# Gated linear attention: operands and outputs moved four chunks at a time, the samples' steps placed between the chunks

## The chip, the core and the metric

The kernel runs on one core of a Trainium2 chip. A core has TensorE (PE), VectorE (DVE), ScalarE (ACT), GpSimd (POOL) and SyncE (SP); each works through its own list of instructions and waits on semaphores for the others. SP, ACT and POOL issue DMAs. The metric is the device time of one execution in microseconds, lower is better.

## What is computed

The whole program is one inference step of two layers for 2048 prompt tokens and 8 sample tokens. The part at issue is the gated linear attention (GLA) of layer 1, four heads with keys of 64 and values of 128. For the prompt it goes in chunks of 64 tokens, 32 of them, one after the other, since each needs the state that the one before leaves:

```
def step(s, inp):
    qi, ki, vi, gi = inp
    b = jnp.cumsum(gi, axis=1)
    inter = jnp.einsum('bthk,bhkv->bthv', qi * jnp.exp(b), s)
    diff = jnp.where(mask, b[:, :, None] - b[:, None, :], -jnp.inf)
    scores = jnp.einsum('bthk,bshk,btshk->bhts', qi, ki, jnp.exp(diff))
    intra = jnp.einsum('bhts,bshv->bthv', scores, vi)
    b_last = b[:, -1]
    k_dec = ki * jnp.exp(b_last[:, None] - b)
    s_new = jnp.exp(b_last)[..., None] * s + jnp.einsum('bshk,bshv->bhkv', k_dec, vi)
    return s_new, inter + intra
```

The 8 samples have one token each: their states are decayed, the product of key and value is added, and the query reads the result. They share nothing with the prompt's chunks but the code.

## The kernel before

The program is a row of stages, each a `with Stage(...)` with its own SBUF and PSUM tensors. A stage ends when all its engines have reached a barrier and its semaphores are cleared, so nothing of the next stage starts earlier. Three stages matter here. `gla_operands` (names `gp_`) writes three operands of all chunks, the scaled query, the scaled key and the key decayed to the chunk's end, to `scratch_gops` in HBM, 128 partitions by 3 operands by 2 pairs of heads by 2048 tokens. `gla_chunks` (`gc_`) runs the 32 chunks. `gla_samples` (`gs_`) does the samples. The stage behind them is the output projection, `Tail` with the names `oo_`.

In `gla_chunks` two heads share the 128 partitions. So the operands of a chunk stand in `opx` as block diagonals: partitions 0 to 63 fill the first 64 columns of each 128x128 block, partitions 64 to 127 the last 64, and the rest stays zero from the memsets at the start. There are `FL` = 4 such buffers. SP fills the buffer of chunk c with two DMAs of 64 partitions each (L2791), as soon as the output products of chunk c-4 are done (`o_pe`). POOL brings the values, `v2`, with two DMAs per chunk under the same rule (L2809).

TensorE's list is written out by hand. In round c it does `scores(c+2)` (L2820, and the transposes of the decayed key, L2828), `state(c+1)` (L2838) and `output(c)` (L2852 and L2853). DVE in round c masks the scores of chunk c+2 (L2899) and updates the state for chunk c (L2913, L2915; it waits there for `output(c-1)`, since the two state buffers alternate). ACT copies the transposed key of chunk c+2 out of PSUM (L2871), then the output of chunk c (L2881), and issues its store (L2883).

`state(c)` waits for the state update of chunk c-2 (`s_sb`, a PSUM buffer is used again), `output(c)` for that of chunk c-1. `scores(c)` waits for the DMAs of its operands. The trace marks the values `v2` and the samples' values both as `v`; in PSUM `gc_b_sc`, `gc_b_kh`, `gc_b_s` and `gc_b_o` are scores, transposed key, state product and output.

In `gla_samples` SP issues 13 loads, DVE runs five large steps and a small one over 128x2048 elements in a row (L2955 to L2960), SP stores the new states, TensorE sums over the key's parts (L2968), DVE copies that (L2962), and SP stores it.

Of the kernel before, what the change touches and what calls it, by code (L numbers as in the profile page):

```python
# [2759 lines left out]
def gla_chunks(nc, ops, v, wc, const, o, s_out):  # L2760
# [3 lines left out]
    FL = 4  # L2764
    with Stage(nc, "gc") as s:
# [3 lines left out]
        ot = [s.sb(f"ot{q}", [P, HD, CH]) for q in (0, 1)]  # L2769
# [5 lines left out]
        ops_in, v_in = ([s.sem(f"{n}{q}") for q in range(FL)] for n in ("ops_in", "v_in"))  # L2775
        o_st = [s.sem("o_st0"), s.sem("o_st1")]
        block = s.block()
# [4 lines left out]
        @block.sync  # L2782
        def _(sp):
            for c in range(NCH):
                q = c % FL
                if c < FL:
                    sp.wait_ge(zero, c + 1)
                else:
                    sp.wait_ge(o_pe, c - FL + 1)
                for r in half:  # L2790
                    sp.dma_start(opx[q][r, :, :, r].rearrange("p n j c -> p (n j) c"),  # L2791
                                 ops[r, :, :, tokens(c)].rearrange("p n j c -> p (n j) c")).then_inc(ops_in[q], 16)
                if c == 0:
                    for dst, src in ((mask[:, :], const["mask4"][:, P:2 * P]), (idt[:, :], const["ident"]),
                                     (wct[:, :, :], wc)):
                        sp.dma_start(dst, src).then_inc(cst, 16)
            sp.wait_ge(s_sb, NCH)
            sp.dma_start(s_out, st[NCH % 2][:, :, :]).then_inc(s_st, 16)
            sp.wait_ge(s_st, 16)

# [12 lines left out]
        def _(pe):  # L2813
            def scores(c):
                q, b = c % FL, c % 2
                pe.wait_ge(ops_in[q], 32 * (c // FL + 1))
# [41 lines left out]
            for c in range(NCH):  # L2858
                if c + 2 < NCH:
                    scores(c + 2)  # L2860
                if c + 1 < NCH:
                    state(c + 1)
                output(c)

        @block.scalar
        def _(act):
            def turned(c):
# [3 lines left out]
                act.copy(kh[c % FL][:, :, :], pair(b_kh[c % 2])).then_inc(kh_ok, 1)  # L2871
            turned(0)
            turned(1)
            for c in range(NCH):
                if c + 2 < NCH:
                    turned(c + 2)
                b = c % 2
                act.wait_ge(o_pe, c + 1)
                if c >= 2:
                    act.wait_ge(o_st[b], 16 * (c // 2))  # L2880
                act.copy(ot[b][:, :, :].rearrange("p n c -> p (n c)"), b_o[b][:, 0:256]).then_inc(o_ev, 1)  # L2881
                act.wait_ge(o_ev, c + 1)
                act.dma_start(o[:, :, tokens(c)].rearrange("n p c -> p n c"), ot[b][:, :, :]).then_inc(o_st[b], 16)  # L2883
            for b in (0, 1):
                act.wait_ge(o_st[b], 16 * NCH // 2)

        @block.vector
        def _(dve):
            for q in range(FL):
                dve.memset(opx[q][:, :, :, :], 0.0).then_inc(zero, 1)  # L2890
            dve.memset(st[0][:, :, :], 0.0).then_inc(zst, 1)
            dve.wait_ge(cst, 48)

            def masked(c):
                q = c % FL
                dve.wait_ge(sc_pe, c + 1)
                if c >= FL:
# [3 lines left out]
                                  ALU.mult).then_inc(sc_ok, 1)  # L2901
            masked(0)
# [14 lines left out]


def gla_samples(nc, vecs, v, state, const, state_out, o):

    BH, KQ = NS * HD, DK // 4
    with Stage(nc, "gs") as s:
        S, T = s.sb("S", [P, KQ, DV]), s.sb("T", [P, KQ, DV])
        vt, vv, yt = s.sb("vec", [P, 3, KQ]), s.sb("v", [P, DV]), s.sb("y", [P, DV])
        yc, sel = s.sb("yc", [P, HD, NS]), s.sb("sel", [P, BH])
        tr = s.ps("tr", [P, 512])
        ready, own, out, y_done, tr_done, yc_done = (s.sem(n) for n in ("ready", "own", "out", "y_done", "tr", "yc"))
        block = s.block()  # L2930
        rows = [slice(BH * n, BH * n + BH) for n in range(4)]
        keys = [slice(KQ * n, KQ * n + KQ) for n in range(4)]

        @block.sync
        def _(sp):
            for n in range(4):
                sp.dma_start(S[rows[n], :, :], state[:, keys[n], :]).then_inc(ready, 16)
                sp.dma_start(vt[rows[n], :, :], vecs.rearrange("n b (h c) -> (b h) n c", c=DK)[:, :, keys[n]]
                             ).then_inc(ready, 16)
                sp.dma_start(vv[rows[n], :], v.rearrange("b (h c) -> b h c", c=DV)).then_inc(ready, 16)  # L2940
            sp.dma_start(sel[:, :], const["sel32"]).then_inc(ready, 16)
            sp.wait_ge(own, 3)
            for n in range(4):
                sp.dma_start(state_out[:, keys[n], :], S[rows[n], :, :]).then_inc(out, 16)
            sp.wait_ge(yc_done, 1)
            sp.dma_start(o[:, :, SEQ:COLS].rearrange("n p c -> p n c"), yc[:, :, :]).then_inc(out, 16)
            sp.wait_ge(out, 80)

        @block.vector
        def _(dve):  # L2950
            link = Chain(dve, own)
            col = lambda n: vt[:, n, :].rearrange("p (k o) -> p k o", o=1).broadcast_to([P, KQ, DV])
            row = vv[:, :].rearrange("p (o v) -> p o v", o=1).broadcast_to([P, KQ, DV])
            dve.wait_ge(ready, 16 * 13)
# [162 lines left out]
```

## Time and profile before

| | us |
|---|---|
| median of 3 runs | 3546.22 (3540.42 to 3549.79) |
| the profiled execution | 3538.04 |
| its span in the trace | 3536.1 |
| first work of `gla_chunks` to first work of `gla_samples` | 3151.09 to 3268.14 |
| first work of `gla_samples` to first work of the output projection | 3268.14 to 3293.73 |

Over the whole span PE is busy 83%, DVE 62%, ACT 34% and POOL 25%. These shares say little of the two stages, which are 4% of the span; there the timeline and the waits are to be read. A row of the timeline has the start, the length, the engine, line and operation, and in brackets how long the engine sat idle before and for what. The length of rows of several matmuls is that of the group. "PEld" is the weight load that goes with each matmul. A float32 matmul shows as two records. A row of the view by stretches has the stretch, its length, the busy us (and instructions) of PE, PEld, DVE, ACT and POOL, PE's granted clock as a share of full speed, the DMA share and GB/s.

### The profile page before, as it was taken

How to read it: one execution, taken by the hardware profiler on the slowest of the kernel's cores; microseconds unless marked ns; L12 is line 12 of the kernel's file. 1: busy time of each engine (PE TensorE's matmuls, PEld its weight loads, DVE VectorE, ACT ScalarE, POOL GpSimd, SP SyncE). 2: the span in 40 equal slices, each digit the busy share in tenths (PEclk: the TensorE clock that was granted, in tenths of full speed). 3: DMA queues.
4: the chain of work that ended last, by engine and by line, in shares of the span. 5: the costliest groups of instructions: out<-in, count | busy, mean ns of one | idle time of the engine just before them, and what ended most of it. 6: DMA issues, size and time to landing. Idle time of an engine off the chain costs nothing. (4 is left out here: it accounts for less than half of the span.)

```text
span 3536.1 us, 77383 instructions
## 1 busy us (share of the span) xinstructions
PE 2921.5 (83%) x31187; PEld 2448.1 (69%) x31187; DVE 2194.1 (62%) x3226; ACT 1215.2 (34%) x2133; POOL 876.6 (25%) x742
## 2 busy tenths in 40 slices
PE   9799999777688853999699999979789989636498
PEld 7699999666677642788588778858656666526376
DVE  3536666486767664776448777521278998652587
ACT  1025555333333313343011110110078888622332
POOL 4100000132333311111211111122166766412211
PEclk9999999888999986999799999989989999869699
DMA  4435545523343426553548999852311010235542
GB/s 158 163 94 151 155 146 152 138 63 92 84 111 89 106 71 187 158 167 108 202 151 294 339 343 340 289 175 95 101 51 61 1 61 13 87 119 126 182 144 91
DMA packets 510629, 500.40 MB, mean 142 GB/s; under 512 B 255105, under 2 KB 404210, under 8 KB 503738
## 3 DMA queue, kind: packets, MB, share of 16 engines
q1 hardware_dynamic: 384794, 336.43, 31.8%
q10 hardware_dynamic: 123440, 154.94, 13.0%
q8 instruction: 244, 4.00, 0.5%
q0 software_dynamic: 2048, 4.20, 0.4%
q14 instruction: 103, 0.84, 0.1%
HBM read 357.25 MB, written 138.41 MB: 140 GB/s over the span
## 5 line engine op out<-in xcount | busy, mean ns | idle before, releaser
L2638 POOL TENSOR_TENSOR sp_att<-sp_beta,sp_left 128x512 f32<-128x512 f32 (+3 forms) x320 | 318.3, 1006 | 197.5 <-DVE sp_left L2594 186.0
L1969 POOL TENSOR_TENSOR rc_ct<-rc_m,rc_lev 128x256 f32<-128x256 f32 x160 | 144.8, 926 | 818.4 <-DVE rc_m L1931 818.4
L102 PE MATMUL po_acc<-po_x_high,po_w_low 128*128 128x412 f32 (+1 forms) x840 | 306.7, 365 | 36.6 <-POOL po_w_low L95 17.9
L102 PE MATMUL pe_acc<-pe_x_high,pe_w_low 128*128 128x412 f32 (+1 forms) x840 | 303.8, 362 | 23.3 <-DVE pe_x_low L95 14.9
L103 PE MATMUL po_acc<-po_x_low,po_w_high 128*128 128x412 f32 (+1 forms) x840 | 299.2, 356 | 0.0
L104 PE MATMUL po_acc<-po_x_high,po_w_high 128*128 128x412 f32 (+1 forms) x840 | 298.9, 356 | 0.0
L104 PE MATMUL pe_acc<-pe_x_high,pe_w_high 128*128 128x412 f32 (+1 forms) x840 | 294.7, 351 | 0.0
L103 PE MATMUL pe_acc<-pe_x_low,pe_w_high 128*128 128x412 f32 (+1 forms) x840 | 294.5, 351 | 0.0
L2594 DVE TENSOR_TENSOR_SCAN sp_left<-sp_z,sp_left,sp_zero 128x512 f32<-128x512 f32 x192 | 235.3, 1266 | 13.6 <-ACT sp_z L2538 11.5
L2325 DVE TENSOR_TENSOR po_work<-po_work,po_q 128x1024 f32<-128x1024 f32 x128 | 175.6, 1372 | 86.2 <-DMA po_work<-in_cache_k 81.0
L102 PEld LDWEIGHTS po_acc<-po_x_high,po_w_low 128*128 128x128 f32 x840 | 162.5, 193 | 84.9 <-ACT po_o L923 32.4
L2530 ACT ACTIVATE sp_beta<-sp_z,sp_bias 128x512 f32<-128x512 f32 (+3 forms) x320 | 183.6, 631 | 74.0 <-PE sp_z L2469 46.5
L923 ACT COPY po_o<-po_acc 128x412 f32<-128x412 f32 (+1 forms) x105 | 52.5, 500 | 396.6 <-PE po_acc L104 369.5
L102 PEld LDWEIGHTS pe_acc<-pe_x_high,pe_w_low 128*128 128x128 f32 x840 | 158.8, 189 | 37.5 <-issue 24.2
L2538 ACT ACTIVATE sp_z<-sp_z,sp_bias_neg 128x512 f32<-128x512 f32 (+3 forms) x320 | 179.8, 614 | 0.0
L2484 PE MATMUL sp_t<-sp_id,sp_att 128*128 128x128 f32 x1088 | 155.9, 282 | 23.4 <-ACT sp_aT L2544 18.8
L1911 ACT COPY rc_lv<-rc_bk 128x512 f32<-128x512 f32 (+2 forms) x160 | 112.8, 715 | 176.1 <-PE rc_bk L1860 145.0
L2484 PEld LDWEIGHTS sp_t<-sp_id,sp_att 128*128 128x128 f32 x1088 | 118.5, 143 | 67.4 <-issue 64.5
L2499 PE MATMUL sp_ob<-sp_aT,sp_v 128*64 128x128 f32 x2176 | 155.4, 282 | 10.0 <-DVE sp_g L2608 10.0
L103 PEld LDWEIGHTS po_acc<-po_x_low,po_w_high 128*128 128x128 f32 x840 | 162.6, 194 | 1.0
L104 PEld LDWEIGHTS po_acc<-po_x_high,po_w_high 128*128 128x128 f32 x840 | 162.3, 193 | 0.7
L103 PEld LDWEIGHTS pe_acc<-pe_x_low,pe_w_high 128*128 128x128 f32 x840 | 158.9, 189 | 1.5
(446 smaller groups left out, 7261.0 us busy)
## 6 DMA issues: line engine op xcount, KB each, us to landing
po_work<-in_cache_k SPq DMA_DIRECT2D x256, 256.0 KB, 5.0
po_work<-in_cache_v ACTq DMA_DIRECT2D x256, 256.0 KB, 4.5
scratch_ops<-pe_work SPq DMA_DIRECT2D x160, 128.0 KB, 2.4
out_z<-pe_o SPq DMA_DIRECT2D x84, 206.0 KB
out_z<-po_o ACTq DMA_DIRECT2D x84, 206.0 KB
pe_w<-in_w_e SPq DMA_DIRECT2D x21, 512.0 KB
po_w<-in_w_o ACTq DMA_DIRECT2D x21, 512.0 KB
rc_opx<-scratch_ops SPq DMA_DIRECT2D x16, 640.0 KB, 5.4
```

What stands on the lines that cost most here:

```text
L102: pe.matmul(out, ll, rh, start=start, stop=False)
L103: pe.matmul(out, lh, rl, start=False, stop=False)
L104: return pe.matmul(out, lh, rh, start=False, stop=stop)
L1911: act.copy(lv[q][:, :, lo:lo + count].rearrange("p s k g c -> p s (k g c)"), b[:, :, 0:count * 2 * CH]).then_inc(u_sb[n], 1)
L1969: pool.tensor_tensor(ct[q][:, n].rearrange("p (s g) c -> p s g c", s=2), m4[q][:, :, :, 0, :], spread(lev[:, n + 1, :]), ALU.mult).then_in ...
L2325: dve.tensor_tensor(kp[:, p % KR], kp[:, p % KR], qb[:, b % 2:b % 2 + 1, :].broadcast_to([P, 2, CW]), ALU.mult).then_inc(prod, 1)
L2484: mm = pe.transpose(tb[h][:, b * P:(b + 1) * P], att[h][:, n % 3, b * P:(b + 1) * P], idt[:, :])
L2499: mm = pe.matmul(ob[tile(n) % 2][c, 0:P], vt[m % 2][:, 4 * g + b, c], aT[h][:, n % 2, b * P:(b + 1) * P], start=(diagonal(n) and b == 0), ...
L2530: act.activation(be[h][:, n % 4, 0:w], zb[h][n % 2][:, 0:w], ACT.Sigmoid, scale=DC ** -0.5, bias=bt[:, head:head + 1]).then_inc(sig[h], 1)
L2538: act.activation(zb[h][n % 2][:, 0:w], zb[h][n % 2][:, 0:w], ACT.Sigmoid, scale=-DC ** -0.5, bias=nbt[:, head:head + 1]).then_inc(kept[h], 1)
L2594: dve.tensor_tensor_scan(row[:, at:at + w][:, ::-1], zb[h][n % 2][:, 0:w][:, ::-1], zero.broadcast_to([P, w]), start, ALU.mult, ALU.add).t ...
L2638: pool.tensor_tensor(att[h][:, n % 3, 0:w], be[h][:, n % 4, 0:w], left[h][tile(n) % 2][:, at + 1:at + 1 + w], ALU.mult).then_inc(at_ok[h], 1)
```

## The change

`gla_samples` is gone as a stage. Its loads, its steps and its stores are in `gla_chunks`.

- SP loads the operands of four chunks with one DMA of 128 partitions into a plain buffer, `raw`, of which there are three; the first group comes in two parts (chunk 0, then chunks 1 to 3). A buffer is used again when the copies out of it are done.
- Out of `raw` two copies per chunk spread the operands over the diagonal blocks of `opx`: DVE partitions 0 to 63, ACT partitions 64 to 127. Both wait for the output products of chunk c-4. `scores(c)` waits for both copies in place of the DMAs. From round 0 on the copies for chunk c+4 stand at the end of DVE's round c and, on ACT, behind the output copy of chunk c.
- ACT gathers the outputs of four chunks in `ot` and issues one store for them.
- ACT issues the samples' 13 loads ahead of its first copy. DVE does the samples' steps at the ends of rounds 4, 6, 8, 10, 12 and 14, the last copy in round 31. SP issues the samples' state stores behind the operand load of chunks 20 to 23. TensorE does the sum between `state` and `output` of the last round, in a PSUM buffer of the transposes.
- POOL's value loads are as they were.

The diff, cut to its core:

```diff
-            for c in range(NCH):
-                q = c % FL
-                if c < FL:
-                    sp.wait_ge(zero, c + 1)
-                else:
-                    sp.wait_ge(o_pe, c - FL + 1)
-                for r in half:
-                    sp.dma_start(opx[q][r, :, :, r].rearrange("p n j c -> p (n j) c"),
-                                 ops[r, :, :, tokens(c)].rearrange("p n j c -> p (n j) c")).then_inc(ops_in[q], 16)
+            for m in range(NCH // 4):
+                q = m % 3
+                if m >= 3:
+                    sp.wait_ge(spread0, 4 * m - 8)
+                    sp.wait_ge(spread1, 4 * m - 8)
...
+                    sp.dma_start(raw[q][:, :, :, :], ops[:, :, :, m * 4 * CH:(m + 1) * 4 * CH]).then_inc(ops_in[q], 16)
+                if m == 5:
+                    sp.wait_ge(own, 3)
+                    for n in range(4):
+                        sp.dma_start(state_out[:, keys[n], :], S[rows[n], :, :]).then_inc(out, 16)
...
-                pe.wait_ge(ops_in[q], 32 * (c // FL + 1))
+                pe.wait_ge(spread0, c + 1)
+                pe.wait_ge(spread1, c + 1)
...
+            def spread(c):
+                q, m = c % FL, c // 4
...
+                if c >= FL:
+                    act.wait_ge(o_pe, c - FL + 1)
+                act.copy(opx[q][half[1], :, :, half[1]], raw[m % 3][half[1], :, :, c % 4 * CH:(c % 4 + 1) * CH]
+                         ).then_inc(spread1, 1)
...
+                act.copy(ot[m % 2][:, :, c % 4 * CH:(c % 4 + 1) * CH], b_o[b][:, 0:256].rearrange("p (n c) -> p n c", c=CH)
+                         ).then_inc(o_ev, 1)
+                if c + 4 < NCH:
+                    spread(c + 4)
+                if c % 4 == 3:
+                    act.wait_ge(o_ev, c + 1)
+                    act.dma_start(o[:, :, m * 4 * CH:(m + 1) * 4 * CH].rearrange("n p c -> p n c"), ot[m % 2][:, :, :]
+                                  ).then_inc(o_st[m % 2], 16)
...
+                dve.tensor_copy(opx[q][half[0], :, :, half[0]], raw[m % 3][half[0], :, :, c % 4 * CH:(c % 4 + 1) * CH]
+                         ).then_inc(spread0, 1)
...
+            def samples(c):
+                if c == 4:
+                    dve.wait_ge(smp, 16 * 13)
+                    dve.tensor_tensor(S[:, :, :], S[:, :, :], col(G_V), ALU.mult).then_inc(own, 1)
...
+                elif c == 12:
+                    dve.wait_ge(own, 4)
+                    dve.tensor_reduce(yt[:, :], T[:, :, :].rearrange("p k v -> p v k"), AX.X, ALU.add).then_inc(own, 1)
...
-def gla_samples(nc, vecs, v, state, const, state_out, o):
```

How the instructions stand on DVE in rounds 4 and 5, before (`L2899` masks, `L2913` and `L2915` update the state):

```order
L2899 TENSOR_TENSOR gc_sc2<-gc_b_sc0,gc_mask 128x256
L2913 SCALAR_TENSOR_TENSOR gc_st1<-gc_st0,gc_wc,gc_b_s0 128x128
L2915 SCALAR_TENSOR_TENSOR gc_st1<-gc_st0,gc_wc,gc_b_s0 128x128
L2899 TENSOR_TENSOR gc_sc3<-gc_b_sc1,gc_mask 128x256
L2913 SCALAR_TENSOR_TENSOR gc_st0<-gc_st1,gc_wc,gc_b_s1 128x128
```

and in the same rounds of the changed kernel:

```order
L2961 TENSOR_TENSOR gc_sc2<-gc_b_sc0,gc_mask 128x256
L2999 SCALAR_TENSOR_TENSOR gc_st1<-gc_st0,gc_wc,gc_b_s0 128x128
L3001 SCALAR_TENSOR_TENSOR gc_st1<-gc_st0,gc_wc,gc_b_s0 128x128
L2950 COPY gc_opx0<-gc_raw2 64x6x64
L2970 TENSOR_TENSOR gc_S<-gc_S,gc_vec 128x2048
L2961 TENSOR_TENSOR gc_sc3<-gc_b_sc1,gc_mask 128x256
L2999 SCALAR_TENSOR_TENSOR gc_st0<-gc_st1,gc_wc,gc_b_s1 128x128
```

A copy into `opx` and, here, the samples' first step of 2048 elements have come between the state update of chunk 4 and the mask of chunk 7.

On ACT, at the stage's start, the queue before begins with its work for chunks 0 and 1:

```order
L2871 COPY gc_kh0<-gc_b_kh0 128x256
L2871 COPY gc_kh1<-gc_b_kh1 128x256
L2871 COPY gc_kh2<-gc_b_kh0 128x256
L2881 COPY gc_ot0<-gc_b_o0 128x256
L2883 DMA scratch_o_d<-gc_ot0 128x4x64
```

and the changed one, from the last four of the samples' 13 loads on:

```order
L2907 DMA gc_S<-in_state_gla 32x2048
L2908 DMA gc_vec<-scratch_gvecs 32x3x16
L2910 DMA gc_v<-out_v1 32x1x128
L2911 DMA gc_sel<-in_sel32 128x32
L2904 COPY gc_opx0<-gc_raw0 64x6x64
L2904 COPY gc_opx1<-gc_raw0 64x6x64
L2894 COPY gc_kh0<-gc_b_kh0 128x256
L2904 COPY gc_opx2<-gc_raw0 64x6x64
L2894 COPY gc_kh1<-gc_b_kh1 128x256
```

The 13 loads and two copies stand ahead of ACT's first copy of a transposed key.

On SP the two loads per chunk,

```order
L2791 DMA gc_opx1<-scratch_gops 64x6x64 x2
L2791 DMA gc_opx2<-scratch_gops 64x6x64 x2
L2791 DMA gc_opx3<-scratch_gops 64x6x64 x2
L2791 DMA gc_opx0<-scratch_gops 64x6x64 x2
L2791 DMA gc_opx1<-scratch_gops 64x6x64 x2
```

have become one per four chunks, with the samples' stores among them:

```order
L2807 DMA gc_raw1<-scratch_gops 128x6x256
L2807 DMA gc_raw2<-scratch_gops 128x6x256
L2807 DMA gc_raw0<-scratch_gops 128x6x256
L2807 DMA gc_raw1<-scratch_gops 128x6x256
L2807 DMA gc_raw2<-scratch_gops 128x6x256
L2811 DMA out_gla_s<-gc_S 32x2048 x4
L2807 DMA gc_raw0<-scratch_gops 128x6x256
```

These loads wait for copies out of `raw`, not for output products.

## Rows read from the trace of the kernel before

**Rows 1.** The view by stretches, of the 100 us of the chunks.

```profile
3163.00:3263.00 100.00, 68.40 (x552) 65.54 (x551) 28.50 (x92) 22.35 (x60) 32.80 (x56) 0.96 0.54 132
```

**Rows 2.** Waits in both stages: who waited for whom, total us, times, longest.

```profile
PE gc_b_sc L2820 <- DMA gc_opx<-scratch_gops: 53.6, 16, 21.5
```

**Rows 3.** Timeline of one pair of chunks and the start of the next.

```profile
3168.55 0.71 PE L2820 MATMUL gc_b_sc<-gc_opx 128*128 128x128 f32 x4 [2.19 <-DMA gc_opx<-scratch_gops]
...
3170.65 0.61 PE L2820 MATMUL gc_b_sc<-gc_opx 128*128 128x128 f32 x4
...
3172.44 0.39 PE L2853 MATMUL gc_b_o<-gc_opx,gc_st 128*128 128x128 f32 x2
3172.86 0.37 ACT L2881 COPY gc_ot<-gc_b_o 128x256 f32<-128x256 f32 x1 [0.77 <-PE gc_b_o L2853]
3173.12 1.17 POOL L2809 DMA_DIRECT2D gc_v<-out_v  x2 [0.83 <-PE gc_b_o L2853]
...
3175.11 0.71 PE L2820 MATMUL gc_b_sc<-gc_opx 128*128 128x128 f32 x4 [2.29 <-DMA gc_opx<-scratch_gops]
```

**Rows 4.** DMA issues of both stages: KB each, median us from issue to landing.

```profile
gc_opx<-scratch_gops SPq DMA_DIRECT2D x64, 96.0 KB, 3.3
gc_v<-out_v POOLq DMA_DIRECT2D x64, 64.0 KB, 3.0
scratch_o_d<-gc_ot ACTq DMA_DIRECT2D x32, 128.0 KB, 3.1
```

**Rows 5.** Groups by form in both stages: count, busy us, mean ns, idle before.

```profile
L2899 DVE TENSOR_TENSOR gc_sc<-gc_b_sc,gc_mask 128x256 f32<-128x256 f32 x32 | 13.6, 425 | 76.5 <-PE gc_b_sc L2820 73.8 <-DMA gc_wc<-scratch_gwc 2.7
L2871 ACT COPY gc_kh<-gc_b_kh 128x256 f32<-128x256 f32 x32 | 11.9, 372 | 75.8 <-PE gc_b_kh L2828 75.0 <-PE gc_b_s L2838 0.8
L2915 DVE SCALAR_TENSOR_TENSOR gc_st<-gc_st,gc_wc,gc_b_s 128x128 f32<-128x128 f32 x32 | 10.9, 341 | 0.0
L2955 DVE TENSOR_TENSOR gs_S<-gs_S,gs_vec 128x2048 f32<-128x2048 f32 x1 | 2.3, 2294 | 14.5 <-DMA gs_sel<-in_sel 14.5
L2959 DVE TENSOR_REDUCE gs_y<-gs_T 128x128 f32<-128x2048 f32 x1 | 3.6, 3578 | 0.0
```

**Rows 6.** Timeline of the chunk stage's start, to the first output products.

```profile
3151.09 3.12 DVE L2890 MEMSET gc_opx<- 128x768 f32 x4 [10.87 <-PEq L72]
...
3158.67 0.93 PEld L2820 LDWEIGHTS gc_b_sc<-gc_opx 128*128 128x128 f32 x4 [1.20 <-DMA gc_opx<-scratch_gops]
...
3162.89 0.55 PEld L2852 LDWEIGHTS gc_b_o<-gc_sc,gc_v 128*128 128x128 f32 x2
```

**Rows 7.** Timeline of the last chunks, the samples and the next stage's start.

```profile
3260.28 0.53 PEld L2838 LDWEIGHTS gc_b_s<-gc_v,gc_kh 128*128 128x128 f32 x4
...
3261.62 0.30 PEld L2852 LDWEIGHTS gc_b_o<-gc_sc,gc_v 128*128 128x128 f32 x2
...
3263.55 0.37 ACTq L2883 DMA_DIRECT2D scratch_o_d<-gc_ot  x1
3268.14 0.34 SPq L2937 DMA_DIRECT2D gs_S<-in_state_gla  x1
...
3274.94 0.44 SPq L2941 DMA_DIRECT2D gs_sel<-in_sel  x1
...
3293.73 0.36 SPq L445 DMA_DIRECT2D oo_ones<-in_all_ones  x1
```

**Rows 8.** Timeline of the program's start: DVE copies beside POOL and without it.

```profile
8.82 9.03 POOL L95 TENSOR_TENSOR pu_w_low<-pu_w,pu_w_high 128x512 fp32r<-128x512 f32 x6 [0.80 <-ACT pu_w_high L322]
...
15.20 1.51 DVE L90 CAST pu_x_high<-pu_x 128x512 fp32r<-128x512 f32 x1
...
18.33 0.41 DVE L90 CAST pu_x_high<-pu_x 128x512 fp32r<-128x512 f32 x1
...
21.52 2.29 DVE L90 CAST pu_x_high<-pu_x 128x4096 fp32r<-128x4096 f32 x1
```

**Rows 9.** DMA issues of the whole program, from the page.

```profile
rc_opx<-scratch_ops SPq DMA_DIRECT2D x16, 640.0 KB, 5.4
```

More of the change, by code:

```diff
@@ L2768, in gla_chunks @@
         sc, kh = four("sc", [P, 2, P]), four("kh", [P, 2, P])
-        ot = [s.sb(f"ot{q}", [P, HD, CH]) for q in (0, 1)]
+        ot = [s.sb(f"ot{q}", [P, HD, 4 * CH]) for q in (0, 1)]
+        raw = [s.sb(f"raw{q}", [P, 3, 2, 4 * CH]) for q in range(3)]
         st = [s.sb(f"st{q}", [P, 2, DV]) for q in (0, 1)]
@@ L2796, in _ @@
                         sp.dma_start(dst, src).then_inc(cst, 16)
+                else:
+                    sp.dma_start(raw[q][:, :, :, :], ops[:, :, :, m * 4 * CH:(m + 1) * 4 * CH]).then_inc(ops_in[q], 16)
[3 more added lines that the diff above has]
+                        sp.dma_start(state_out[:, keys[n], :], S[rows[n], :, :]).then_inc(out, 16)
+            sp.wait_ge(yc_done, 1)
+            sp.dma_start(o[:, :, SEQ:COLS].rearrange("n p c -> p n c"), yc[:, :, :]).then_inc(out, 16)
             sp.wait_ge(s_sb, NCH)
@@ L2799, in _ @@
             sp.wait_ge(s_st, 16)
+            sp.wait_ge(out, 80)
         @block.gpsimd
@@ L2862, in _ @@
                     state(c + 1)
+                if c == NCH - 1:
+                    pe.wait_ge(y_done, 1)
+                    pe.wait_ge(kh_ok, NCH)
+                    pe.matmul(b_kh[0][:, 0:BH], yt[:, :], sel[:, :], start=True, stop=True).then_inc(tr_done, 1)
                 output(c)
@@ L2891, in _, with spread @@
             dve.memset(st[0][:, :, :], 0.0).then_inc(zst, 1)
+            def spread(c):
+                q, m = c % FL, c // 4
+                if c == 0:
+                    dve.wait_ge(zero, FL)
+                    dve.wait_ge(first_in, 16)
+                else:
+                    dve.wait_ge(ops_in[m % 3], 16 * (m // 3 + 1))
+                if c >= FL:
+                    dve.wait_ge(o_pe, c - FL + 1)
+                dve.tensor_copy(opx[q][half[0], :, :, half[0]], raw[m % 3][half[0], :, :, c % 4 * CH:(c % 4 + 1) * CH]
+                         ).then_inc(spread0, 1)
+            for c in range(FL):
+                spread(c)
             dve.wait_ge(cst, 48)
@@ L2916, in _ @@
                                          in1=b_s[b][:, DV:2 * DV], op0=ALU.mult, op1=ALU.add).then_inc(s_sb, 1)
-def gla_samples(nc, vecs, v, state, const, state_out, o):
[L2923 to L2954, printed above, removed]
-            dve.tensor_tensor(S[:, :, :], S[:, :, :], col(G_V), ALU.mult)
-            link(dve.tensor_tensor(T[:, :, :], row, col(G_K), ALU.mult))
-            link(dve.tensor_tensor(S[:, :, :], S[:, :, :], T[:, :, :], ALU.add))
-            link(dve.tensor_tensor(T[:, :, :], S[:, :, :], col(G_Q), ALU.mult))
-            link(dve.tensor_reduce(yt[:, :], T[:, :, :].rearrange("p k v -> p v k"), AX.X, ALU.add))
-            dve.tensor_scalar(yt[:, :], yt[:, :], DK ** -0.5, None, ALU.mult).then_inc(y_done, 1)
-            dve.wait_ge(tr_done, 1)
-            dve.tensor_copy(yc[:, :, :], tr[:, 0:BH].rearrange("v (b h) -> v h b", h=HD)).then_inc(yc_done, 1)
-        @block.tensor
-        def _(pe):
-            pe.wait_ge(ready, 16 * 13)
-            pe.wait_ge(y_done, 1)
-            pe.matmul(tr[:, 0:BH], yt[:, :], sel[:, :], start=True, stop=True).then_inc(tr_done, 1)
@@ L2971, in program @@
+                if c + 4 < NCH:
+                    spread(c + 4)
+                samples(c)
 def program(nc, I, O):
```

61 lines of the change are left out of this document (49 added, 12 removed).

## The prediction

> **What bounds the kernel now.** I read three views in this order. First the view by stretches, since the shares of the whole span say nothing of a stage that is 3% of it: in the 100 us of the chunks PE is busy 68%, DVE 29%, ACT 22%, POOL's issues 33%, and the granted clock is 0.96, so nearly all of it is at the 2.4 GHz level [rows 1]. No engine is full. So a wait sets the pace, and the view of waits names it: PE waits 53.6 us, 16 times, for the DMAs of `opx`; one of these, 21.5 us, is the stage's start, which leaves about 2.1 us each for the others [rows 2]. The timeline shows the form [rows 3]: scores at 3168.55 and 3170.65, the last output product at 3172.44, then nothing until 3175.11. A pair of chunks takes 6.56 us, 4.1 of it work. The loop behind it: output products of chunk c-4, two issues on SP, 3.3 us to landing [rows 4], scores of chunk c. The scores stand two rounds ahead of the output products of their chunk, so the loop spans two rounds and closes once per pair.
>
> The samples' stage, 3268.14 to 3293.73, is serial: 13 issues, DVE's steps, stores, 25.6 us in all, with nothing beside it [rows 7].
>
> **A round when nothing waits.** At full clock a round's 18 matmul records follow each other at 0.111 us: from 3170.65 to 3172.44 plus the last group's two is 2.01 us [rows 3]. So PE alone would give 2.00 us per chunk, against about 3.3 now.
>
> **What the change does to the loop over the chunks.** Take the start of the output products of chunk 0 to that of chunk 31: 3162.89 [rows 6] to 3261.62 [rows 7], 98.7 us. With PE never waiting it is one output (8 records, 0.89), 29 full rounds (58.0), round 30, which has no scores (3260.28 to 3261.62, 1.34 [rows 7]), and the samples' sum (some 0.3): 60.5 us. **-38.2 us.** I go through what could be late next, with zero at the end of the output products of chunk c.
>
> *The copies.* On DVE a copy of 64x384: copies of 128x512 and 128x4096 between SBUF tensors took 0.41 and 2.29 us [rows 8], which is 0.52 ns a column, so 0.35 us. On ACT, 128x256 takes 0.372 us [rows 5]; with 384 columns 0.5 is my estimate. Both start at zero and are due when PE comes to `scores(c+4)`, two rounds on, at 4.0. The round of DVE is 0.425 + 2 x 0.341 + 0.35, about 1.46 us; that of ACT 0.37 + 0.37 + 0.5 and a quarter of a store, about 1.4 [rows 5]. Both fit into 2.0. The state update of chunk c+1 has slack as well, since masks and updates are due more than a round later. So the copies cost nothing while PE's round covers them; without that cover each would cost its 0.35 or 0.5 us per chunk.
>
> *The samples' steps.* Four steps of 2.29 us and one of 3.58 [rows 5] stand in DVE's list behind the copy, and behind each are queued the mask of chunk c+3 and the state update of chunk c+1. PE's `state(c+3)` waits for that update. Two rounds of DVE with a step in one of them take 2 x 1.46 + 2.29 = 5.2 us, against PE's 4.0: +1.2, four times; with the reduction 6.5 against 4.0: +2.5. Together **+7.3 us**. Bounds: +4 if the steps find slack, +9 if the copies take 0.5.
>
> *The values.* POOL's loads are unchanged, but the rounds are shorter. The values of chunk c are issued after the output products of c-4: POOL starts 0.46 us after PE's end (3173.12 against 3172.66), the second issue 0.59 later [rows 3], and lands 3.0 us on [rows 4]: 4.05 us. They are due at `state(c)`, two rounds and six records later, 4.67 us. Slack 0.6 us. It bounds the pace from a landing of 3.6 us on. The nearest rows are 3.0, 3.1 and 3.3 [rows 4], the farthest 5.4 for a 640 KB load [rows 9]; the same bytes in 2.0 us instead of 3.3 means more traffic, in longer pieces and in bursts of 768 KB. I take the nearest rows with an occasional late one, **+1.5 us**; at 4.0 us to landing the round would be 2.2, +5.5 us; at 5.4, 2.9, +27.
>
> *Operands and stores.* A group of four is due every 8 us or more, and is asked for when the copies of the group three back are done, about two groups ahead; 5.4 us [rows 9] fits. Nothing. The samples' stores on SP wait for a DVE step of round 8; the load for chunks 20 to 23 stands ahead of them. Nothing.
>
> **The start.** Now the stage starts at 3151.09, the scores of chunk 1 at 3158.67 and the first output products at 3162.89, 4.2 us later [rows 6]. In the change ACT first issues 13 loads. On SP these took from 3268.14 to 3275.38, 7.24 us [rows 7]. So ACT is free at 3158.3, its first copy ends at 3158.8, the scores of chunk 1 follow 1.2 us behind those of chunk 0 at the slow clock, at 3160.05. Plus 4.2: 3164.3. **+1.4 us** (0 if PE's clock rises sooner, +3 if issues beside those of SP and POOL are slower).
>
> **The end.** From the last output store's issue to the next stage are 4.6 us now [rows 7], 3.1 of them the landing of 128 KB [rows 4]. The store is now 512 KB; between 3.1 and 5.4 I take 4.3, and the wait for an older store ahead of the last copy (0.5) goes: **+0.7 us** (-0.5 to +2). The samples' stage goes whole, with its barrier: **-25.6 us** (3268.14 to 3293.73 [rows 7]). What it did is in the terms above.
>
> **Sum.** -38.2 + 7.3 + 1.5 + 1.4 + 0.7 - 25.6 = -52.9 us. The profiled execution of 3538.0 us would be 3485.1. It lies 8.2 us under the median of the runs shown, 3546.2; by the median the forecast is 3493.3 us.
>
> **A page that speaks against it.** The shared port first as rows show it: at the program's start DVE's copy of 128x512 took 1.51 us while POOL was at work from 8.82 to 17.85, and 0.41 us once it was idle [rows 8]. The Trainium skill's page "SBUF — State Buffer", section "SBUF: two separate sides", says that a float32 `tensor_copy` within SBUF locks GpSimd out of the shared pair, so that a DMA issued from there waits for its descriptors until the copy's end. The values' loads are such DMAs, and now DVE copies at just the moment when POOL issues them. By that rule their landing moves by 0.1 to 0.2 us, inside the slack of 0.6, and the sum stays. Its other direction, POOL holding DVE, is rival B.
>
> **Rivals.**
> A (0.20), *the values' loads set the pace*: landing 4.0 to 4.4 us, rounds of 2.2 to 2.4, +5.5 to +11 on the forecast, about 3501. For it: slack of only 0.6 us, and denser traffic. Against: longer pieces.
> B (0.12), *POOL's issues hold up DVE's copies*: both are released by the same output products. ACT started 0.03 us after their end, POOL 0.29 [rows 3]; if DVE starts like ACT it is first. If it is late, the copy waits for both issues, 1.17 us, and DVE's round is 1.46 + 1.17 = 2.6: +0.6 in 29 rounds, +18, about 3511. For it: 1.51 against 0.41 us [rows 8].
> C (0.05), *the wait for operands stays* (the change doesn't do what it says): groups of 768 KB land later than the 8 us that they are due in, 3520. Against: 5.4 us for 640 KB [rows 9].
> D (0.02), *slower*: without the samples' stage the loop could grow by 27 us before all is lost, that is to rounds of 4.2 us instead of 3.3. One mechanism reaches that: the values' loads, starved behind the bursts, land in over 8 us (0.46 + 0.59 + 8 - 0.67 over two rounds). At 9 us rounds are 4.2 to 4.7: 3560. Against: no row here has such a landing for 64 KB.
> The likeliest case, PE's own pace with DVE's steps showing, 0.61.
>
> **How the numbers follow.** The likeliest gives 3493. Its own range takes the bounds of the terms, -59 to -45, and 5 us of scatter of the runs: 3482 to 3506. A reaches into it, B to 3511. Up to 3512 some 0.15 are left out on both sides together, so 3482 to 3512. A measurement can tell about 0.3% of this kernel, 10.6 us, from no change. All cases but C's tail and D are faster by more: faster 0.97, same 0.01, slower 0.02.
>
> **What would show it.** Right: in the chunks PE over 90% busy outside rounds 4 to 14, scores every 2.0 us, five gaps of 1 to 2.5 us put down to DVE's state update, first output products near 3164, the output projection near 3241 in the trace. PE waiting for `v` at `b_s` in most rounds would be A; copies of 0.35 us lengthened to over 1 us, B; copies that wait for `raw`, C. The forecast is wrong if rounds differ from 2.0 by more than 0.3 us, or if ACT's 13 issues take much more than 7 us.

## The result, and the profile after

The changed kernel takes 3503.08 us (median of 4, 3494.02 to 3508.46), the kernel before 3544.56 beside it. The ratio is 0.9885, with a 95% interval of 0.9868 to 0.9902. By the medians it is 41.5 us faster, by the ratio 1.15%. The forecast was 3493, range 3482 to 3512.

The stage is read best by its own marks, since the rest of the program moves by several microseconds from one execution to the next: its first issue came at 3151.09 before and comes at 3159.30 now, though nothing ahead of it was changed. From that issue to the output projection's first were 142.6 us [rows 6, 7]; now they are 100.2 us (3159.30 to 3259.51). That is 42.4 us less where 52.9 were forecast. The start answers to [rows 6]; this is the timeline of the changed kernel:

```profile
3159.30 0.54 SPq L2801 DMA_DIRECT2D gc_raw<-scratch_gops  x1
3159.31 0.37 ACTq L2907 DMA_DIRECT2D gc_S<-in_state_gla  x1
...
3161.87 0.44 SPq L2805 DMA_DIRECT2D gc_wc<-scratch_gwc  x1
...
3167.63 0.47 ACTq L2911 DMA_DIRECT2D gc_sel<-in_sel  x1
3168.19 0.51 ACT L2904 COPY gc_opx<-gc_raw 64x384 f32<-64x384 f32 x1 [25.51 <-issue]
...
3173.84 0.69 PE L2847 MATMUL gc_b_kh<-gc_id,gc_opx 128*128 128x128 f32 x2 [3.80 <-DMA gc_wc<-scratch_gwc]
...
3178.38 0.47 PEld L2871 LDWEIGHTS gc_b_o<-gc_sc,gc_v 128*128 128x128 f32 x2
```

The first output products come 19.1 us after the stage's first issue, before 11.8. Two things stand in the way: ACT's 13 issues, 8.8 us long (3159.31 to 3168.10), and after them the constants, which SP issued by 3162.31 and which have not landed at 3173.

The loop itself, in PE's timeline. These are the groups at which PE idled, and one pair of scores rows for the pace; they answer to [rows 3]:

```profile
3183.56 0.61 PE L2839 MATMUL gc_b_sc<-gc_opx 128*128 128x128 f32 x4
...
3185.57 0.61 PE L2839 MATMUL gc_b_sc<-gc_opx 128*128 128x128 f32 x4
...
3191.39 0.68 PE L2857 MATMUL gc_b_s<-gc_v,gc_kh 128*128 128x128 f32 x4 [0.98 <-DVE gc_st L3001]
...
3195.02 0.68 PE L2857 MATMUL gc_b_s<-gc_v,gc_kh 128*128 128x128 f32 x4 [1.39 <-ACT gc_kh L2894]
...
3202.25 0.68 PE L2857 MATMUL gc_b_s<-gc_v,gc_kh 128*128 128x128 f32 x4 [0.98 <-DVE gc_st L3001]
...
3206.11 0.68 PE L2857 MATMUL gc_b_s<-gc_v,gc_kh 128*128 128x128 f32 x4 [1.62 <-ACT gc_kh L2894]
...
3215.06 0.68 PE L2857 MATMUL gc_b_s<-gc_v,gc_kh 128*128 128x128 f32 x4 [2.42 <-DVE gc_st L3001]
...
3229.20 0.68 PE L2857 MATMUL gc_b_s<-gc_v,gc_kh 128*128 128x128 f32 x4 [1.60 <-ACT gc_kh L2894]
```

Where nothing waits the round is 2.01 us, as worked out. Two kinds of gap remain, both ahead of a state product. Those put down to `gc_st` (0.98, 0.98, 2.42) are the samples' steps. Those put down to ACT's `gc_kh` (1.39, 1.62, 1.60, chunks 8, 12 and 20) need care: a state product waits for the key, the values and an older state, and the profile names what came last by its own marks. The DMA view of two short stretches, KB and us to landing, says more. First the values issued at 3182.02, then those at 3188.03, when a group of operands and an output store were under way:

```profile
gc_v<-out_v POOLq DMA_DIRECT2D x2, 64.0 KB, 2.2
```

```profile
gc_v<-out_v POOLq DMA_DIRECT2D x2, 64.0 KB, 5.8
```

From the issues at 3188.03 (the second 0.59 later) 5.8 us lead to 3194.4 or so; PE's group begins at 3195.02. A landing of 3.6 us had been the limit.

After the gap of 2.42 us the granted clock fell. The view by stretches, columns as in [rows 1], of the 3 us behind it and of a stretch near the end:

```profile
3217.00:3220.00 3.00, 3.00 (x17) 3.00 (x16) 1.39 (x5) 1.15 (x3) 1.17 (x2) 0.55 0.15 44
```

```profile
3230.00:3245.00 15.00, 14.56 (x130) 14.27 (x130) 9.03 (x28) 8.77 (x21) 8.18 (x14) 1.00 0.45 129
```

At 0.55 nearly all of it is the 1.2 GHz level; two rounds took 2.87 and 2.85 us, 1.7 more than at 2.4 GHz. In the second stretch PE is busy 97%, and over the whole loop (3178.4 to 3254.5) 86%, against 68% over the chunks before [rows 1].

The copies, in the view of groups by form (count, busy us, mean ns), beside POOL's issues of the values:

```profile
L2904 ACT COPY gc_opx<-gc_raw 64x384 f32<-64x384 f32 x32 | 16.3, 508 | 27.1 <-issue 25.5 <-DMA gc_raw<-scratch_gops 0.8
L2950 DVE COPY gc_opx<-gc_raw 64x384 f32<-64x384 f32 x32 | 11.2, 356 | 28.1 <-PE gc_b_o L2872 22.0 <-DMA gc_raw<-scratch_gops 6.1
L2827 POOL DMA_DIRECT2D gc_v<-out_v x64 | 37.6, 593 | 140.9 <-POOLq L72 89.2 <-PE gc_b_o L2872 51.6
```

And the end, which answers to [rows 7]:

```profile
3255.23 0.37 ACTq L2931 DMA_DIRECT2D scratch_o_d<-gc_ot  x1
3259.51 0.34 SPq L445 DMA_DIRECT2D oo_ones<-in_all_ones  x1
```

4.3 us from the last store's issue to the next stage, before 4.6.

### The profile page after: what moved, and what is told of

Its sections match the earlier page's. It is cut to its first block and busy times, and to the rows that moved or that the text cites. A ratio compares the mean times of both kernels' runs of the same rounds, so it can differ in the third digit from the quotient of the medians.

```text
span 3500.9 us, 77385 instructions
## 1 busy us (share of the span) xinstructions
PE 2929.3 (84%) x31187; PEld 2458.2 (70%) x31187; DVE 2202.9 (63%) x3258; ACT 1230.8 (35%) x2165; POOL 876.4 (25%) x742
## 3 DMA queue, kind: packets, MB, share of 16 engines
q10 hardware_dynamic: 111712, 156.09, 13.2%
q0 software_dynamic: 2048, 4.20, 0.5%
```

## The experiments

Theory at the outset: what is missing of the forecast lies in ACT's issues and late constants at the start (5.9 us), in values that land late beside a burst of operands, and in the clock behind the longest gap; the samples' steps cost what was forecast. Rivals: the first 15 us are filled by the bytes themselves, in whatever order; PE waits for ACT, as the profile's column says; DVE's work counts however it is cut.

All marks are in us and good to 0.1. "First scores" and "first output" count from the stage's first issue; "loop" runs from the start of the first weight load for an output to the start of the last one (0.7 to 0.8 us more than between the starts that the forecast used); "stage" ends with the output projection's first issue. Each row is one profiled execution. Kernels with a ratio were timed in four executions against the kernel before, the others once. The rows come from four comparisons, in which the median of the kernel before lay between 3539.29 and 3544.56 us, so times of different rows are compared by their ratios.

| kernel | first scores | first output | loop | stage | time | ratio to before |
|---|---|---|---|---|---|---|
| before | 4.3 | 11.8 | 99.5 | 142.6 | 3544.56 | 1 |
| changed | 9.5 | 19.1 | 76.0 | 100.2 | 3503.08 | 0.9885 (0.9868 to 0.9902) |
| changed, again | 9.6 | 19.5 | 79.2 | 103.8 | 3494.48 | 0.9869 (0.9847 to 0.9890) |
| constants first | 8.7 | 15.2 | 79.3 | 99.6 | 3497.55 | |
| constants first, loads on SP | 4.0 | 12.5 | 79.8 | 97.5 | 3498.26 | 0.9889 (0.9857 to 0.9920) |
| eight value buffers | 9.2 | 16.9 | 75.0 | 97.1 | 3490.35 | 0.9865 (0.9839 to 0.9891) |
| steps in quarters | 9.3 | 18.5 | 75.4 | 99.0 | 3497.20 | |
| groups of four only | 4.0 | 12.2 | 72.1 | 115.1 | 3511.01 | 0.9905 (0.9886 to 0.9925) |
| operand loads of one chunk | 9.4 | 18.8 | 72.3 | 96.6 | 3492.08 | |
| both copies on ACT | 9.7 | 16.6 | 73.7 | 95.5 | 3494.08 | |
| all four edits | 4.0 | 12.5 | 68.9 | 86.6 | 3490.41 | 0.9839 (0.9814 to 0.9863) |
| all four, steps from round 8 | 4.0 | 13.2 | 63.3 | 81.7 | 3480.48 | 0.9832 (0.9816 to 0.9849) |
| the same, third group held back | 4.0 | 13.1 | 62.5 | 81.8 | 3485.33 | 0.9842 (0.9823 to 0.9861) |

**The changed kernel again.** No edit.

> The changed kernel again, unaltered, for the scatter of the stage's length in the trace from one execution to the next: 100.2 us in the first profile; between 98 and 102 expected, with the stalls for late values at the same chunks 8, 12 and 20 and three gaps of DVE's samples' steps.

103.8 us, outside the range expected; the stalls stand at the same chunks, but those of chunks 20 and 27 are 2.27 and 1.80 us in place of 1.60 and 0.44, and the clock falls once more behind the first. So a stage length of a single profile is uncertain by some 4 us, nearly all of it in the loop; the marks at the start repeat within 0.5 in these two. They move more in the kernels with eight value buffers and with both copies on ACT: SP's list is that of the changed kernel there, but PE waited 2.48 and 1.64 us for the constants in place of 3.80 and 4.24, and the first output came at 16.9 and 16.6. Below, a difference in the loop under 4 us decides nothing by itself, and the gaps are read one by one.

**Constants first.**

```diff
                     sp.dma_start(raw[0][:, :, :, 0:CH], ops[:, :, :, 0:CH]).then_inc(first_in, 16)
+                    for dst, src in ((mask[:, :], const["mask4"][:, P:2 * P]), (idt[:, :], const["ident"]),
+                                     (wct[:, :, :], wc)):
+                        sp.dma_start(dst, src).then_inc(cst, 16)
                     sp.dma_start(raw[0][:, :, :, CH:4 * CH], ops[:, :, :, CH:4 * CH]).then_inc(ops_in[0], 16)
```

> The changed kernel, with SP's three loads of constants (mask, identity, decays) issued right behind the operands of chunk 0 and ahead of those of chunks 1 to 3. In the changed kernel's trace PE has the scores of chunk 0 at 3168.85 and then waits 3.8 us for the last constant. Theory 1 (the constants are late because they queue behind 576 KB on SP's own queue): that wait falls to 0 to 0.5 us, the operands of chunk 1 become what PE waits for at most briefly, and the stage (100.2 us from its first issue to the next stage's) is 3 to 4 us shorter, 96 to 97 us. Rival (they are late because all queues together fill the DMA engines in the first 15 us): the wait moves to the operands of chunk 1 or stays within 1 us of what it was, stage 99 to 100 us.

PE no longer waits for the constants; the operands of chunk 1 hold it 0.70 us. The first output comes 3.9 us sooner, which is the theory's size, though the two kernels named above came 2.2 and 2.5 us sooner without this edit, so the size is uncertain by as much. The stage became 0.6 us shorter and no more, since the loop was longer, with value stalls at chunks 4, 19, 20 and 27 that were absent or shorter before. So it is shown that the constants were late by their place in the queue, and a gain of the stage is not shown.

**Constants first, and the samples' loads on SP.** The 13 `act.dma_start` lines move behind the third group of operands on SP:

```diff
-            for n in range(4):
-                act.dma_start(S[rows[n], :, :], state_in[:, keys[n], :]).then_inc(smp, 16)
...
+                if m == 2:
+                    for n in range(4):
+                        sp.dma_start(S[rows[n], :, :], state_in[:, keys[n], :]).then_inc(smp, 16)
```

> As the run with the constants first, and in addition the samples' 13 loads are issued by SP behind the third group of operands in place of ACT at its start. Theory 1: ACT's 13 issues (8.8 us, 3159.3 to 3168.1) held the first copy into the diagonal blocks; without them the first scores start about 5 us after the stage's first issue in place of 9.5, and the first output products at 11 to 12 us in place of 19.1; stage 92 to 94 us, time 0.2% below that of the changed kernel. Rival (the start is held by the DMA engines, which the same bytes fill whoever issues them): the first scores come sooner but the operands of chunk 1 land as late as before (at 10.2 us), first output products at 15 us or later, stage 96 us or more.

First scores at 4.0 us, first output at 12.5: the start is as it was before the change, so both causes of the late start are confirmed, ACT's issues and the constants. The stage was 97.5, not 92 to 94, and the ratio, 0.9889, is no better than the changed kernel's. PE's timeline shows where the rest went:

```profile
3163.43 1.19 PE L2846 MATMUL gc_b_sc<-gc_opx 128*128 128x128 f32 x4 [2.68 <-DVE gc_opx L2951]
...
3178.66 1.19 PE L2864 MATMUL gc_b_s<-gc_v,gc_kh 128*128 128x128 f32 x4 [4.95 <-issue]
```

A stall of 4.95 us at the fifth state product, the first whose values are issued inside the loop while groups of operands and the samples' states are coming in. These values landed 8.6 us after their issue at 3169.33. The rival was wrong on the start, which it put at 15 us or later, and right on the stage, 96 us or more: a start without its holds meets the burst sooner and waits there.

**Eight value buffers.**

```diff
-                q = c % FL
-                if c >= FL:
-                    pool.wait_ge(o_pe, c - FL + 1)
+                q = c % 8
+                if c >= 8:
+                    pool.wait_ge(o_pe, c - 8 + 1)
```

> The changed kernel with eight buffers for the values in place of four, so that the loads of a chunk's values are issued four rounds sooner. In the changed kernel's trace PE stalls 1.39, 1.62 and 1.60 us ahead of the state products of chunks 8, 12 and 20, and 0.4 us at 19 and 27; the profile names ACT's copy of the transposed key, which had long been done. Theory 1 (values that land late, 5.8 us beside a 768 KB group of operands, 2.2 us without): all five stalls go, 5.5 us, stage about 95 us; the stalls of DVE's samples' steps in rounds 6 and 10, hidden behind those waits so far, come out with about 1 us each, so the net is 3 to 5.5 us. Rival (ACT is late with the transposed keys, as the profile says): the stalls stay and the stage stays at 100 us.

In PE's waits no row with ACT's `gc_kh` is left, and of the stalls ahead of state products those by the samples' steps stand alone:

```profile
PE gc_b_s L2857 <- DVE gc_st L3001: 6.6, 5, 2.7
PE gc_b_kh L2847 <- DMA gc_wc<-scratch_gwc: 2.5, 1, 2.5
PE gc_b_sc L2839 <- DVE gc_opx L2950: 2.3, 1, 2.3
```

So those stalls were the values, not ACT: ACT's work did not change. The five gaps of DVE are 0.98 four times and 2.69 once, in rounds 4 to 12, 6.6 us, against 7.3 forecast. The loop gained only 1 us, less than the scatter. PE met a late second group of operands (2.3 us, ahead of the scores of chunk 4) in place of late values, with a low clock behind it; from one state product to the next it took 4.58 and 3.68 us there.

**Steps in quarters.** Each long step becomes four, `S[:, k, :]` with `k` four of the 16 keys (for the reduction, 32 of 128 values), one at the end of each of rounds 4 to 23.

> The changed kernel with each of the samples' five long steps on DVE cut into four, one quarter at the end of each of rounds 4 to 23 (the small scaling in round 24, the state's store three groups later). A quarter is about 0.6 to 0.65 us, so a round of DVE is 1.46 + 0.65 = 2.1 us against PE's 2.0. Theory 1 (the steps stall PE because a round of DVE with one is 3.7 to 5.1 us long, and the gap of 2.4 us behind the reduction also costs some 2 us of slow clock): the gaps of 1.0, 1.0 and 2.4 us and the slow stretch at 3216 to 3220 go, the rounds are 2.0 to 2.2 us; stage 95 to 97 us. Rival (DVE's total work counts however it is cut): the 13 us of steps push out as many small gaps, stage 99 to 101 us.

No gap of PE is put down to `gc_st` any more, and no low clock follows the reduction. A quarter takes 0.68 us, of the reduction 1.03. In their place stand longer stalls for values (1.54, 1.32, 1.30, 1.16, 1.92 at chunks 8, 12, 16, 19 and 20). All gaps of the loop together are 10.5 us, as in the changed kernel (10.3), and the stage, 99.0, is in the rival's range. But the rival's reason does not hold: with eight value buffers beside them (the steps from round 8 on, below) the same quarters leave no gap that is put down to DVE's state update. With one cause left in, removing the other shows little.

**Groups of four alone.** The samples are a stage of their own again, and all their lines are out of `gla_chunks`.

> One part alone: operands and outputs in groups of four with the copies, the samples as a stage of their own as before the change. Theory: PE's own pace with the late values as the only stalls. First output products at 13 to 16 us (no loads of the samples on ACT; constants still behind the operands), the loop 66 to 70 us (60.5 of work, the stalls of late values 5 us), samples' stage 25.6 us again; from the first issue of the chunks to the output projection 110 to 114 us, against 142.6 before and 100.2 with both parts; the median some 30 us under the kernel before. Rival (the saving came mostly from merging the samples): 125 us or more.

115.1 us, 1 us over the range: first output at 12.2, loop 72.1. So of the 42.4 us the groups bring 27.5 (142.6 to 115.1) and the merging 14.9 (115.1 to 100.2), though it removes a stage of 25.6: it costs 6.9 at the start and 3.9 in the loop. The split is uncertain by the 4 us between the two profiles of the changed kernel. By the times the groups bring 33.3 us, and the merging 8 to 12 more (41.5 and 44.8 us for the changed kernel in its two comparisons). PE's value stalls without any of the samples' traffic:

```profile
PE gc_b_s L2850 <- ACT gc_kh L2883: 4.8, 5, 1.2
PE gc_b_s L2850 <- issue: 3.4, 4, 1.8
```

That is 8.2 us, against 5.9 in the changed kernel, where the gaps of the samples' steps stand in front of some of them.

**Operand loads of one chunk.**

```diff
-                    sp.dma_start(raw[q][:, :, :, :], ops[:, :, :, m * 4 * CH:(m + 1) * 4 * CH]).then_inc(ops_in[q], 16)
+                    for e in range(4):
+                        sp.dma_start(raw[q][:, :, :, e * CH:(e + 1) * CH],
+                                     ops[:, :, :, (m * 4 + e) * CH:(m * 4 + e + 1) * CH]).then_inc(ops_in[q], 16)
```

> The changed kernel with each load of four chunks' operands (768 KB, pieces of 1 KB) replaced by four loads of one chunk (192 KB, pieces of 256 B), issued together. Question: what makes the values land after 5.8 us in place of 2.2. Theory 1 (whatever bytes of operands are in flight on SP's queue share the DMA engines with the values, so only amount and piece size count): short pieces make it worse, values' landing beside a group 6 us or more, stalls at the state products of chunks 8, 12, 20 of 2 us or more each, stage 101 to 106 us. Rival (it is the single large transfer): the stalls shrink, values' landing under 4.5 us, stage 96 to 98 us.

My theory was wrong here. With pieces of 256 B the values landed in 4.9 us at most (medians of stretches of 3 us) with operands under way, where it was 5.8, and the DMA view of the stage gives:

```profile
gc_raw<-scratch_gops SPq DMA_DIRECT2D x29, 192.0 KB, 4.6
gc_v<-out_v POOLq DMA_DIRECT2D x64, 64.0 KB, 3.7
```

3.7 in the median of 64 against 3.9. Value stalls fell from 5.9 to 1.8 us in all. The loop fell to 72.3, in one profile and by less than the scatter. What the edit can't separate is the size of a piece from that of a transfer; which of them it is stays open.

**Both copies on ACT.** DVE's copy is taken out, ACT makes both.

> The changed kernel with ACT making both copies into the diagonal blocks and DVE none. It tests the shared port: POOL issues a chunk's values while DVE copies. In the changed kernel's trace, values issued in stretches without other traffic land 2.2 us after their issue, POOL's issue takes 0.592 us and DVE's copy 0.352. If DVE's copies held back the descriptors (the rule of the Trainium skill's page SBUF, State Buffer, section SBUF: two separate sides), the landing in quiet stretches falls below 2.1 us and the issue gets shorter; if not (theory 1), 2.2 us and 0.592 stay within 0.05 us. The round of ACT grows by 0.5 to about 1.9 us, just under PE's 2.0, so the stage may lose 1 to 8 us to ACT; DVE's gaps at the samples' steps shrink from 0.98 to about 0.3 us.

In stretches with neither operands nor stores under way the values land in 2.2 to 2.3 us, as with DVE's copies, and POOL's issue takes 594 ns, against 593. So neither copy nor issue is seen to hold the other up. ACT's fuller round cost nothing that shows: the stage was 95.5 us, with DVE's largest gap down from 2.42 to 1.37. The other gap put down to DVE was 0.85, not the 0.3 expected.

**All four edits together.**

> All four edits together: constants first, the samples' loads on SP behind the third group, eight value buffers, the samples' steps in quarters. If each stall is its own cause, the stage has its first output products at 12 to 13 us, a loop of 62 to 66 us and 5 us of tail: 80 to 84 us against 100.2, the median 15 to 20 us under that of the changed kernel (0.981 to 0.984 of the kernel before). Rival (what the start gains, the loop gives back, since the same bytes must come in during the first 25 us; so far the two edits of the start gained 3.9 and 6.6 us there and the loop was 3.3 and 3.8 us longer): stage 88 us or more.

86.6 us, between the two ranges; the ratio, 0.9839, is inside the one that was expected. After the start one gap is left. DVE's timeline shows it, here with the state update that PE waits for:

```profile
3185.96 0.69 DVE L2980 TENSOR_TENSOR gc_S<-gc_S,gc_vec 128x512 f32<-128x512 f32 x1 [5.38 <-DMA gc_sel<-in_sel]
3186.57 0.42 DVE L2962 TENSOR_TENSOR gc_sc<-gc_b_sc,gc_mask 128x256 f32<-128x256 f32 x1
3186.91 0.34 DVE L3006 SCALAR_TENSOR_TENSOR gc_st<-gc_st,gc_wc,gc_b_s 128x128 f32<-128x128 f32 x1
```

The samples' steps wait for their own loads, which now come in behind the operands, and mask and state update are queued behind them: PE idles 4.86 us.

**The steps from round 8 on.**

```diff
-                step, part = divmod(c - 4, 4)
+                step, part = divmod(c - 8, 4)
```

> The four edits together with the samples' quarters four rounds later (rounds 8 to 27, the scaling in round 28). In the trace of the four edits together one gap of 4.86 us is left in the loop: DVE waits 5.38 us in round 4 for the last of the samples' loads, which SP issued 13 us after the stage's start, and the state update of chunk 5 is queued behind it; the clock is low for some 2 us afterwards. Theory: without it the loop is 61 to 63 us in place of 68.9 and the stage 79 to 81 us; median 5 to 7 us under that of the four edits. Rival (another late transfer takes its place, such as the operands of chunk 4 or 8): stage 83 us or more.

81.7 us and a loop of 63.3 (62.5 between the starts that the forecast used), against the 60.5 that PE's work alone comes to; both are just over what was expected. One gap over 0.3 us is left in it, 1.24 us at 3189.10, ahead of scores whose operands came in late. The view by stretches of 40 us in the middle:

```profile
3190.00:3230.00 40.00, 40.00 (x360) 39.93 (x360) 35.62 (x99) 24.25 (x59) 16.41 (x28) 1.00 0.68 194
```

PE is busy throughout at full clock, with 360 records in 40 us, which is the 0.111 us of the forecast; DVE is busy 89%. The time is 3480.48 us, 0.9832 of the kernel before, 14.0 us under the changed kernel in the same comparison. It is the lowest ratio of all, though those of the kernels in the rows above and below it, 0.9839 and 0.9842, lie inside its interval: the 5 to 7 us that this edit was to bring are seen in the stage (4.9), and in the time not clear of the noise.

**The third group held back.** SP waits for DVE's first copy ahead of it.

> As the run with the quarters from round 8, and SP holds the third group of operands (and the samples' loads behind it) back until DVE has made its first copy. In the four edits' trace PE waits 2.6 us at the start for the operands of chunk 1 (576 KB issued beside two groups of 768 KB). Theory (they share the DMA engines with the groups behind them on the same queue): with a third less in flight that wait is 1.5 to 2 us, the stage 0.5 to 1 us shorter. Rival (one queue serves its transfers mostly in order, so what is behind does not matter): the wait stays at 2.6 us within 0.3, the stage the same within 0.5 us or longer.

The wait for chunk 1 was 3.23 us, in the kernel without the hold 3.39, and the stage was the same too (81.8). But the edit hardly did what it was meant to: DVE's first copy ended 3.8 us after the stage's first issue, and without the hold the third group had been issued at 3.4. It was under way in both kernels for most of the time until chunk 1's operands landed (8.2 us). And the wait for chunk 1 was 2.60 us in the kernel with all four edits, whose start is the same as without the hold. So whether transfers behind it in its queue slow a load stays open.

## Why the prediction came out as it did

The time fell into the range, 10 us on the slow side of the forecast, close to rival A's 3501. That is in part luck: the 42.4 us saved between the stage's first issue and the next stage's are outside the forecast's own bounds (45 to 59), and the range held it because it had been widened for the rivals and the scatter. Of the signs that the prediction had named, the round of 2.0 us and the copies' lengths came; of the five gaps of DVE three showed; ACT's issues took 8.8 us where more than 7 was to count against it; and counted from the stage's first issue the output projection begins at 100.2 us and not at 89.7 (142.6 less 52.9). By its steps:

**What bound the kernel** was right: the loop over the operands' DMAs. PE's wait for them is gone from the loop, and the round without a wait is 2.01 us.

**The start failed**: +1.4 forecast, +7.3 measured (11.8 to 19.1). The term had ACT's issues at 7.24 us, from rows in which SP issued alone; beside SP's and POOL's they took 8.8. Its bound of +3 would have covered that. What it left out altogether are the constants. They were third in SP's queue behind 192 KB, they are now behind 768 KB, and PE's transposes wait for them, 3.80 us. Putting them ahead ended that wait and brought 3.9 us back there. The step missing was one that the forecast's own method asks for: what the transfers of the start are queued behind.

**The samples' steps** were right in mechanism and size: 6.6 us with nothing in front of them (4 x 0.98 + 2.69), 7.3 forecast. In the changed kernel itself only 4.4 show, in rounds 4, 8 and 12; those of rounds 6 and 10 coincide with late values.

**The values** had the right mechanism, the right limit (3.6 us) and too small a size: +1.5 forecast. The gaps at chunks 8, 12 and 20 alone are 4.6 us, in the second profile 5.0 (1.19, 1.57, 2.27). With the three short ones (chunks 19, 27 and 31) they are 5.9 us of idle time; by the lengths of the rounds, which also hold what PE loses in starting again, 7.1. The landing was taken at 3.0 us on average, where it is 2.2 in quiet and up to 5.8 beside a burst. So it's not a pace, as rival A had it, but a stall about once in a group of four.

**The clock** was in no term for the loop: 1.7 us behind the gap of 2.42 us. The loop went from 98.7 (3162.89 to 3261.62) to 75.3 us (3178.38 to 3253.63), where 69.3 were forecast. By the lengths of the rounds that is 60.5 of work, 4.9 for the samples' steps, 7.1 for the values and 1.7 for the clock, 74.2 in all; the remaining 1.1 are small amounts in other rounds. So the term that was mis-sized in the loop is that of the values.

**The copies** took 0.356 and 0.508 us, forecast 0.35 and 0.5, and PE's round covers them. **Operands and stores**: groups landed in 7.8 us in the median, not 5.4, and were still in time within the loop. Once values are early enough, the operands are what is late next (2.3 us with eight buffers). **The end**: -0.6 in place of +0.7. From the start of the last output products to the next stage it took 6.5 us before and 5.9 now, since the last 512 KB landed sooner than the 4.3 us assumed; the median of such stores is 3.4.

In the sum, 5.9 us of the missing 10.5 are the start, 5.9 the loop, and the end gives 1.3 back. **Rival B** is ruled out: of DVE's 32 copies the longest was 0.514 us, the stage's first, beside POOL's first eight issues, and the median is 0.352; with the constants first, that copy took 0.35 beside the same issues. As for the shared port, DVE's copy starts at 3245.71 and lasts 0.35 us, and POOL's issue starts at 3245.90, inside it; yet in quiet stretches the values land in 2.2 us with DVE's copies and in 2.2 to 2.3 without. By the rule of the Trainium skill's page "SBUF — State Buffer", section "SBUF: two separate sides", the descriptors would wait for the copy's end, which by these rows is 0.16 us, my estimate. No such wait shows here, in a view that gives tenths of a microsecond; a longer copy was not tried.

Of the rivals it remains true that values come late (A), in stalls and not as a pace. That the groups' traffic is what makes them late rests on when they are late, and on the shorter landings with loads of one chunk; the output stores under way in some of the same stretches were not taken away by themselves. The samples' traffic was, and the stalls stayed (groups of four alone). It is also open why some stalls vary from one execution to the next.

## What to carry to other kernels

When a wait for a DMA is removed from a loop, list every other transfer that the loop needs and its slack at the new pace; an average landing time hides a burst once per group, and here four more buffers removed those stalls. Work that is moved beside a loop comes with its loads, and both ends must be checked: what its issues stand ahead of, and whether it waits for loads that now come late. Where two causes stall the same instruction in turn, removing one at a time shows almost nothing (1 to 3 us of stage each here, less than the scatter); removing them together gave 18.5 us of stage and 14.0 us of time.

## What the runs showed of the hardware

- A 64 KB load issued by POOL landed in 2.2 us alone, in 5.8 beside a 768 KB load in pieces of 1 KB on SP's queue and a 512 KB output store, and in at most 4.9 in the run with loads of 192 KB in pieces of 256 B, four at a time. I had expected short pieces to make it worse.
- Small loads wait for large ones ahead of them in the same queue: constants of 160 KB behind 768 KB were not in after 11 us; when they were issued ahead of 576 KB of those, PE did not wait for them.
- In this loop the granted clock fell to 1.2 GHz for some 3 us behind gaps of 2.27, 2.32, 2.42 and 2.69 us, and not behind those of 0.4 to 2.03 us. The length of the gap alone does not tell: in the run with the constants first and the loads on SP it stayed at 2.4 GHz behind one of 2.70 us (3210.61), and in the kernel before it stayed there behind twelve gaps of 2.10 to 2.35 us and fell behind one of 2.05 (3201.05) and one of 2.65 (3228.95). Why it falls behind one and not behind another is open.
- The same 13 loads took 7.24 us to issue from SP alone and 8.8 from ACT while SP and POOL issued too. An issue of one 256 KB load took 0.34 to 0.44 us in the first case and up to 1.32 in the second; with all four edits, on SP behind the first loads of operands, 2.53.
